# Two decoder layers on one core: first loads put in one queue, two modulation products moved, the attention output product split

## The reference

```python
c_act = silu(c)
for i in range(2):
    mod = c_act @ ada_w[i] + ada_b[i]                      # 6 x 1024
    shift_m, scale_m, gate_m, shift_f, scale_f, gate_f = split(mod, 6)
    h = rmsnorm(x, norm_g[i, 0]) * (1 + scale_m) + shift_m
    y = s5_mixer(h, ...) if i == 0 else stick_breaking_attention(h, w_qkv, w_out)
    x = x + gate_m * rmsnorm(y, norm_g[i, 1])
    h = rmsnorm(x, norm_g[i, 2]) * (1 + scale_f) + shift_f
    y = swiglu(h, ...) if i == 0 else moe_swiglu(h, ...)   # 8 experts, top 2
    x = x + gate_f * rmsnorm(y, norm_g[i, 3])
```

## Time and profile before

| | |
|---|---|
| Time before, median of 3 runs | 1456.86 us (1450.53 to 1460.29) |
| The profiled execution: device time | 1458.7 us |
| The profiled execution: span of its instructions | 1456.9 us |
| PE busy | 1336.3 us, 92% of the span |
| DVE / ACT / POOL busy | 657.1 / 510.7 / 41.7 us |
| DMA queue of SP (q1) | 470.83 MB, 78.3% of 16 engines' span |
| HBM read | 471.48 MB, 324 GB/s over the span |

### The profile page before, as it was taken

The page is one execution under the profiler, slowest core; times in us unless marked ns, Lnnn a source line. Parts: engine busy times, 40 slices in busy tenths (PEclk is TensorE's granted clock), DMA queues, the critical chain, the costliest instruction groups (busy, mean ns, idle before and its releaser), DMA issues.

```text
span 1456.9 us, 25193 instructions
## 1 busy us (share of the span) xinstructions
PE 1336.3 (92%) x11110; PEld 955.9 (66%) x11111; DVE 657.1 (45%) x738; ACT 510.7 (35%) x559; POOL 41.7 (3%) x80
## 2 busy tenths in 40 slices
PE   2999999999999888999999899999898899988776
PEld 1774678888779754677777677777676666644332
DVE  4943354444453444555554665554765463200002
ACT  1323433433344432444443444443454352000001
POOL 3000000000010003000000000000000000000000
PEclk8989999999999998999999999999999899999999
DMA  9573794555485305679999979999999999999994
GB/s 398 226 320 134 295 406 174 180 200 198 174 322 196 118 7 224 239 286 389 422 429 430 428 284 387 424 428 429 429 398 429 430 428 430 427 431 431 430 431 185
DMA packets 33371, 474.29 MB, mean 326 GB/s; under 512 B 3682, under 2 KB 3810, under 8 KB 4578
## 3 DMA queue, kind: packets, MB, share of 16 engines
q1 hardware_dynamic: 32544, 470.83, 78.3%
q10 hardware_dynamic: 706, 1.72, 0.3%
HBM read 471.48 MB, written 1.05 MB: 324 GB/s over the span
## 4 chain that ended last, share of the span: by engine, by line
PE 76%; DMA 17%; DVE 3%; ACT 2%; issue 1%; POOL 1%; ACTq 0%; POOLq 0%; SPq 0%; DVEq 0%
PE ps L2394 42%; PE ps L2725 10%; DMA ring<-in_moe_w_down_dram 8%; DMA ring<-in_moe_w_gate_up_dram 6%; PE ps L2737 6%; DMA arena<-in_s_cb_dram 2%; PE ps L2567 2%; PE ps L2370 2%; PE ps L2212 1%; DMA ring<-in_ada_w_dram 1%; PE ps L2717 1%; PE ps L2646 1%; PE ps L2269 1%; PE ps L2659 1%; PE ps L2707 1%
## 5 line engine op out<-in xcount | busy, mean ns | idle before, releaser
L1962 DVE TENSOR_TENSOR ring_lo<-ring,w 128x2048 fp32r<-128x2048 f32 x122 | 278.9, 2290 | 165.9 <-ACT w L1100 129.3
L1100 ACT ACTIVATE w<-ring 128x2048 fp32r<-128x2048 f32 x122 | 232.8, 1912 | 193.4 <-PE ps L2394 192.0
L2725 PE MATMUL ps<-ring,arena 128*32 128x128 f32 (+1 forms) x5376 | 239.3, 292 | 24.6 <-DMA ring<-in_moe_w_gate_up_dram 20.0
L2725 PEld LDWEIGHTS ps<-ring,arena 128*32 128x32 f32 (+1 forms) x5376 | 183.3, 114 | 84.5 <-DMA ring<-in_moe_w_gate_up_dram 30.4
L2394 PE MATMUL ps<-ring_lo,x_hi 128*128 128x512 f32 x576 | 224.7, 390 | 0.0
L1592 DVE TENSOR_TENSOR ring_lo<-ring,w_hi 128x2048 fp32r<-128x2048 f32 x42 | 95.6, 2290 | 86.5 <-ACT w_hi L822 86.5
L2394 PE MATMUL ps<-w,x_hi 128*128 128x512 f32 x320 | 128.8, 402 | 1.3 <-DVE arena L1914 1.1
L2394 PE MATMUL ps<-w,x_lo 128*128 128x512 f32 x320 | 124.8, 390 | 0.0
L2394 PEld LDWEIGHTS ps<-ring_lo,x_hi 128*128 128x128 f32 x576 | 108.3, 188 | 20.7
L822 ACT ACTIVATE w_hi<-ring 128x2048 fp32r<-128x2048 f32 x42 | 78.8, 1909 | 46.6 <-PE ps L2394 42.1
L2737 PE MATMUL ps<-ring,tri 128*32 128x512 f32 (+1 forms) x448 | 72.2, 650 | 23.0 <-DMA ring<-in_moe_w_down_dram 21.0
(11 more groups left out here) (397 smaller groups left out, 1695.2 us busy)
## 6 DMA issues: line engine op xcount, KB each, us to landing
ring<-in_moe_w_gate_up_dram SPq DMA_DIRECT2D x112, 2048.0 KB, 15.0
ring<-in_moe_w_down_dram SPq DMA_DIRECT2D x56, 2048.0 KB, 16.9
ring<-in_ada_w_dram SPq DMA_DIRECT2D x24, 2048.0 KB, 9.9
ring<-in_ffn_w_gate_up_dram SPq DMA_DIRECT2D x14, 2048.0 KB, 11.0
ring<-in_ffn_w_down_dram SPq DMA_DIRECT2D x7, 2048.0 KB, 8.6
ring<-in_sb_w_qkv_dram SPq DMA_DIRECT2D x6, 2048.0 KB, 8.7
ring<-in_s_w_out_dram SPq DMA_DIRECT2D x2, 2048.0 KB, 8.8
ring<-in_sb_w_out_dram SPq DMA_DIRECT2D x2, 2048.0 KB, 14.3
```

What stands on the lines that cost most here:

```text
L1100: act.activation(half3(h).bitcast(F32R), ff_half(gran(pair_place(*main_granule(n))), half), ACT.Copy).then_inc(whi_done, 1 + h if h and h ...
L1962: dve.tensor_tensor(ff_half(ring_lo[place % RING][:, :], half).bitcast(F32R), ff_half(gran(place), half), half3(h), ALU.subtract).then_inc ...
L2725: ins = pe.matmul(dst[width * r:width * r + width, 0:cols], x[:, k, 0:width], weights[:, k, cols * r:cols * r + cols], start=k == 0, stop= ...
```

## The change

Three places of the program are changed.

1. SP issues `x_sb` and then both S5 matrices (now one array of 128 x 1024, `cb`, one DMA) ahead of its first weight granule; ACT issues only `small` and the bias. The two blanks are ACT copies with scale 0 (`blank`) in place of POOL memsets. PE turns the groups of `bs` as 2, 4 and 2: two ahead of `ada_fold(1)`, two in the middle of `h @ w_in`. DVE starts the angles (two instructions) ahead of `hT_evict(0)`.
2. Between the S5 mixer and the FFN, `transpose_x(1)` goes ahead of `ada(6)`, which now uses PSUM bank 2 and whose fold goes into the FFN's first block; `ada(7)` and its fold go there too.
3. In the attention output product, three of four weight halves and `oT` are split; the first half of the first granule stays plain.

```diff
+            sp.dma_start(x_sb[:, :, :], x[0].rearrange("(t p) d -> p t d", p=P)).then_inc(x_in, 16)
+            sp.dma_start(cb, s5_cb).then_inc(cb_in, 16)
             for r in range(4):
...
-            pool.memset(ring[:, RING - 2, :], 0.0).then_inc(blank_done, 1)
-            pool.memset(resp.rearrange("p i t d h -> p (i t d h)"), 0.0).then_inc(blank_done, 1)
...
-            act.dma_start(x_sb[:, :, :], x[0].rearrange("(t p) d -> p t d", p=P)).then_inc(x_in, 16)
-            act.dma_start(cT.rearrange("p i t h -> p (i t h)"), s5_cb[0]).then_inc(cb_in, 16)
-            act.dma_start(b_raw.rearrange("p i t h -> p (i t h)"), s5_cb[1]).then_inc(cb_in, 16)
...
+            def blank(dst, columns):
+
+                src = ones[:, :].unsqueeze(1).to_broadcast([P, columns // P, P])
+                act.activation(dst.rearrange("p (a b) -> p a b", b=P), src, ACT.Copy, scale=0.0).then_inc(blank_done, 1)
+
+            blank(ring[:, RING - 2, :], GRAN)
...
+            blank(resp.rearrange("p i t d h -> p (i t d h)"), 2 * NT * (CHUNK + 1) * 32)
...
             ada_part(1)
+            wv_out(0, 2)
             ada_mod(1)
-            wv_out(0, 4)
+            wv_out(2, 4)
             hT_evict(0)
-            wv_out(4, 8)
+            wv_out(4, 6)
             u_raw_out(0)
+            wv_out(6, 8)
...
-            ada_part(7)
+            ada_part(6)
             for f in range(FB):
...
                 if f == 0:
-                    ada_mod(7)
+                    ada_mod(6)
                 silu_out(f, 1)
                 if f:
                     a_round(2 * f - 1, 0)
+                else:
+                    ada_part(7)
                 w_round(g + 1, 1)
+                if f == 0:
+                    ada_mod(7)
...
+            def s_round(h):
+
+                wait_landed(act, N_SBOUT + h // 2)
+                if h == 3:
+                    act.wait_ge(o_ps, HEADS // 2)
+                act.activation(half_s(h).bitcast(F32R), ff_half(gran(N_SBOUT + h // 2), h % 2), ACT.Copy
+                               ).then_inc(s_whi, 1)
...
+                if h == HEADS // 2:
+                    s_round(1)
...
+            o_round(0)
+            s_round(2)
+            o_round(1)
+            s_round(3)
             wait_used(act, N_SBOUT + 1)
...
+            angles(True)
             hT_evict(0)
-            angles()
+            angles(False)
...
+            s_rest(1)
             gate_diag(2)
+            o_rest(0)
+            o_rest(1)
+            s_rest(2)
             gate_copy(2)
+            s_rest(3)
...
+            pe.wait_ge(ct_done, 8)
+            turned_bs(0, 2)
             ada_fold(1)
...
+            turned_bs(2, 6)
             wait_hT(0)
...
                 if b == 1:
                     ins.then_inc(u_ps, 1)
+                    turned_bs(6, 8)
...
             ada_fold(4)
-            pe.wait_ge(mod_out, 5)
-            ada(6)
             ada_fold(5)
             transpose_x(1)
-            ada_fold(6)
-            pe.wait_ge(mod_out, 6)
-            ada(7)
+            ada(6)
             wait_hT(1)
...
                 if f == 0:
-                    ada_fold(7)
+                    ada_fold(6)
+                    ada(7)
...
                 if f == 0:
+                    ada_fold(7)
                     pe.wait_ge(mod_out, 8)
...
+            wait_landed(pe, N_SBOUT)
+            for tt in range(TT):
+                for k in range(KD // 2):
+                    pe.matmul(ps[:, Y_BANK + 2 * tt, :], oT[:, k, P * tt:P * tt + P], gran8(N_SBOUT)[:, k, :],
+                              start=k == 0, stop=False)
+            gate_row(2)
+            pe.wait_ge(s_olo, 2)
+            for h in range(1, 4):
+                r, half = divmod(h, 2)
+                pe.wait_ge(s_wlo, h)
```

More of the change, by code:

```diff
@@ L238, in program @@
         par = pl(42, NT)
-        cT = pl(2, NT, HG)
         rows = pl(640)
@@ L888, in _ @@
             ada_mod(5)
-            ada_part(6)
-            ada_mod(6)
             def a_round(q, ch):
@@ L974, in _, with o_round @@
                     act.preload_act_table_set("natural_log_exp_and_others")
+            def s_round(h):
[4 more added lines that the diff above has]
+                               ).then_inc(s_whi, 1)
+            def o_round(half):
+                k = slice(4 * half, 4 * half + 4)
+                act.wait_ge(o_done, 4 * half + 4)
+                act.activation(x_hi[:, k, :].bitcast(F32R), oT[:, k, :], ACT.Copy).then_inc(s_ohi, 1)
             for h in range(HEADS // 2 + 1):
                 b = h % 2
+                if h == HEADS // 2:
+                    s_round(1)
                 if h < HEADS // 2:
@@ L1426, in y_banks, with angles @@
                 return ps[:, Y_BANK + 2 * tt:Y_BANK + 2 * tt + 2, :].rearrange("p a b -> p (a b)")
-            def angles():
+            def angles(begin):
                 dve.wait_ge(turn_ready, 2)
@@ L1435, in angles @@
                 s, co = sinT, cosT
-                step(dve.tensor_tensor(s, t, fh, ALU.mult))
-                link(dve.tensor_tensor(co, t, fl, ALU.mult))
+                if begin:
+                    step(dve.tensor_tensor(s, t, fh, ALU.mult))
+                    link(dve.tensor_tensor(co, t, fl, ALU.mult))
+                    return
                 link(dve.tensor_scalar(scratch, s, MAGIC, MAGIC, ALU.add, ALU.subtract))
@@ L1710, in _, with s_rest, o_rest @@
             o_out(HEADS // 2 - 1)
+            def s_rest(h):
+                dve.wait_ge(s_whi, h)
+                dve.tensor_tensor(low_s(h).bitcast(F32R), ff_half(gran(N_SBOUT + h // 2), h % 2), half_s(h), ALU.subtract
+                                  ).then_inc(s_wlo, 1)
+            def o_rest(half):
+                k = slice(4 * half, 4 * half + 4)
+                dve.wait_ge(s_ohi, half + 1)
+                dve.tensor_tensor(x_lo[:, k, :].bitcast(F32R), oT[:, k, :], x_hi[:, k, :], ALU.subtract).then_inc(s_olo, 1)
+            s_rest(1)
             gate_diag(2)
+            o_rest(0)
+            o_rest(1)
+            s_rest(2)
             gate_copy(2)
+            s_rest(3)
             wait_used(dve, N_SBOUT + 1)
@@ L2252, in _, with turned_bs @@
             ada(1)
-            ada_fold(1)
-            pe.wait_ge(ct_done, 8)
-            for m in range(8):
-                i, q = divmod(m, TPB)
-                pe.wait_ge(bs_done, i + 1)
-                above(pe, wv_done, m - 1)
-                for t in range(TPB):
-                    ins = pe.transpose(ps[:, 2 + m % 2, P * t:P * t + P],
-                                       bs[:, i, TPB * q + t, :, :].rearrange("p d h -> p (d h)"), ident[:, :])
-                ins.then_inc(bt_ps, 1)
+            def turned_bs(lo, hi):
+                for m in range(lo, hi):
+                    i, q = divmod(m, TPB)
+                    pe.wait_ge(bs_done, i + 1)
+                    above(pe, wv_done, m - 1)
+                    for t in range(TPB):
+                        ins = pe.transpose(ps[:, 2 + m % 2, P * t:P * t + P],
+                                           bs[:, i, TPB * q + t, :, :].rearrange("p d h -> p (d h)"), ident[:, :])
+                    ins.then_inc(bt_ps, 1)
+            pe.wait_ge(ct_done, 8)
+            turned_bs(0, 2)
+            ada_fold(1)
+            turned_bs(2, 6)
             wait_hT(0)
@@ L2561, in _ @@
             pe.wait_ge(o_done, HEADS // 2)
-            for r in range(2):
-                n = N_SBOUT + r
-                wait_landed(pe, n)
-                for tt in range(TT):
-                    for k in range(KD):
-                        ins = pe.matmul(ps[:, Y_BANK + 2 * tt + r, :], oT[:, k, P * tt:P * tt + P], gran8(n)[:, k, :],
-                                        start=k == 0, stop=k == KD - 1)
-                    if r == 0 and tt == 0:
-                        gate_row(2)
-                ins.then_inc(used[n % RING], 1)
+            wait_landed(pe, N_SBOUT)
[8 more added lines that the diff above has]
+                pe.wait_ge(s_wlo, h)
+                hi, low = [w.rearrange("p (k n) -> p k n", n=512) for w in (half_s(h), low_s(h))]
+                for tt in range(TT):
+                    t = slice(P * tt, P * tt + P)
+                    for i in range(KD // 2):
+                        k = KD // 2 * half + i
+                        ins = split_product(ps[:, Y_BANK + 2 * tt + r, :], (x_hi[:, k, t], x_lo[:, k, t]),
+                                            (hi[:, i, :], low[:, i, :]), k == 0, k == KD - 1)
+                if half:
+                    ins.then_inc(used[(N_SBOUT + r) % RING], 1)
             ada(10)
@@ L3239, in laid_out @@
     b = [inputs[f"s5_b_{part}"][0].reshape(NT, 2, NS, HG).transpose(1, 2, 0, 3) for part in ("re", "im")]
-    s5_cb = np.stack([np.concatenate([w.reshape(P, NT * HG) for w in pair], axis=1) for pair in (c, b)])
+    s5_cb = np.concatenate([w.reshape(P, NT * HG) for w in c + b], axis=1)
     def by_columns(w, width):
```

13 lines of the change are left out of this document (10 added, 3 removed).

## The result

The changed kernel takes 1444.85 us (median of 17 runs, 1441.22 to 1450.35), the kernel before 1455.84 (17 runs beside them, 1448.44 to 1462.00). The ratio is 0.993, with a 95% interval from 0.9913 to 0.9947: 10.2 us less, between 7.7 and 12.7. That lies inside the range of 1433 to 1449, 4.85 us above the 1440 forecast. By the bound of 1% it is "within 1%" (chance 0.40) and not "faster" (0.57), which I had held the likelier, and the sum of 16.7 us lies outside the measured 7.7 to 12.7. The profiled execution has a span of 1440.4 us, 16.5 less than the profiled one of before and almost exactly that sum. The agreement is an accident in two ways. Two effects of about 6 us that the sum didn't have stand against each other in it, as the experiments show.

What follows compares the result with a forecast made beforehand. The prediction took the expert stretch as a fixed-length block, PE and weight stream tied together, hanging on the routing. From a median of 1456.86 us, -10.0 - 2.5 - 4.2 = -16.7 gave 1440.2, said as 1440, range 1433 to 1449.

Steps and rivals of the forecast that it cites:

- the bound of 1%: What a measurement of this kernel can tell from no change: 14.6 us, a time of 1442.3 us.
- the sum of 16.7 us: Whole kernel: gains of 10.0 at the start, 2.5 in the modulation products and 4.2 in the output product.
- Step 1, the start: Kernel start: x and matrices land earlier, `h @ w_in` starts 11.1 us earlier; -10.0 us after 1.1 for turning inside it.
- Rival C: Kernel start: landing order does not follow the queue, so the start gains nothing; 1450 us, chance 0.05.
- rival B: Start gives half, -6.5: `small` lands no earlier or `ada(1)` at low clock delays ACT; sum -13, 1444, chance 0.20.
- Step 2, the modulation: Between mixer and FFN: FFN starts 6.4 to 8.1 us earlier but takes on 4.8; net -2.5 us taken.
- Step 3, the output product: Attention output product: 24 of 32 matmuls split, 25.2 us for 29.46, -4.2 us.
- Behind it the same length: Expert stretch: routing comes 16 to 17 us earlier and the stretch behind it keeps its length.
- Rival F: Expert stretch lasts longer by what is saved, needing a stream ahead of the routing; no change, 1457, chance 0.03.
- Rival D: PE clock: idle at 27 to 33 us goes, low clock near 96 us later or shorter; 5 us more, 1435, chance 0.08.
- rule on transposes: Kernel start: transposes don't count as busy PE for the clock, so `h @ w_in` would begin at 1.2 GHz.

Runs made afterwards that it cites:

- experiment 8: Kernel before with only the loads of x and the S5 matrices moved first in SP's queue: 1447.40 us, ratio 0.9935.
- experiment 1: Kernel before with the start part alone (queue order, blanks on ACT, split turning of `bs`, earlier angles): 1440.67 us, ratio 0.9898.
- experiment 5: Kernel before with 49 fulfilled waits ahead of PE's first product, no work changed: 1467.15 us, ratio 1.0058.
- 6: Changed kernel with 209 fulfilled waits ahead of PE's first product, with its own 47 making a shift of 256: 1441.86 us, ratio 0.9907.
- 9: Changed kernel with 112 fulfilled waits ahead of `ada(0)`, branches 159 instructions further than before: 1437.64 us, ratio 0.9888.
- 12: Kernel before with the output product split alone and 110 fulfilled waits ahead of `ada(0)`: 1448.21 us, ratio 0.9937.
- experiment 2: Kernel before with the modulation part alone (x turned ahead of `ada(6)`, `ada(7)` inside the first FFN block): 1455.06 us, ratio 0.9999.
- 3: Kernel before with the split output product alone: 1457.74 us, ratio 1.0021.
- 7: Changed kernel with 197 fulfilled waits and three extra products into an unused bank ahead of `ada(1)`: 1446.49 us, ratio 0.9933.
- experiment 10: Changed kernel with 209 instructions at the end of an unexecuted body of the first expert pair, moving the branch target: 1444.59 us, ratio 0.9936.
- 11: Changed kernel with three extra products into an unused bank ahead of `ada(1)`, without added waits: 1448.13 us, ratio 0.9950.
- experiment 4: The whole changed kernel measured again beside its three parts on one chip, against the kernel before: 1445.15 us, ratio 0.9927.

## Why the prediction was right in time and wrong in its account

- **Step 1, the start: right.** x at 6.1 us (6.9 worked out), the matrices at 7.3 (8.1), `ada(1)` at 27.68 (27.9), `h @ w_in` at 39.53 (38.3, inside 37.3 to 39.8). Its end came 8.8 earlier where the sum has 10.0: `ada(1)` took 6.51 us, more than the 5.44 of the low clock in the earlier trace rows that I had taken as the worst. Rival C is refuted by experiment 8. The measured time is that of rival B (1444), but not for its reason: it had the start at -6.5, and PE's rows have -8.8. Its second half, a slow `ada(1)` that delays ACT, did happen and cost the 1.2 us.
- **Step 2, the modulation: too large.** -1.4 for -2.5 in the profile. Where the start part is there nothing of it is left: experiment 1, without the modulation part, reaches the third FFN product at 158.9, since `ada(7)` ran at the full clock there. The sum compared with products of 5.34 us in the earlier trace rows, whose length was the clock's and not the order's.
- **Step 3, the output product: right in its own rows**, 25.23 us for 25.2 and no wait. The price that the sum left out is what it adds to the instruction stream.
- **"Behind it the same length": the step that failed.** I took the expert stretch as a block of fixed length that hangs on the routing, so the sum put its change at nothing. It lost 6.5 us of the 23.0 in the profiles, about as much as the sum of 16.7 lies above the measured 10.2, though what part of that is the clock's isn't known. Rival F named that outcome, but for another reason, a weight stream running ahead, and SP's wait is still 25.8 us. What is shown: the large gaps come with 49 instructions and no other change (experiment 5) and go with a shift to 256 (6) or 159 (9, 12), and the small gap moves by half as many products as instructions were put ahead. That the gaps are fetches of instructions is inferred from this. The Trainium skill (Runtime: NRT & Kernel Launch, "Instruction fetch mechanics") says that instructions are refilled in blocks of 16 KiB, 256 of them, and that "Branching breaks sequential prefetch". The traces agree: the instruction queue moved 1.51 MB in 92 packets, 16.4 KB each, and 256 instructions bring the old gaps back. If so, the branch hints in the code hide the fetch only from some places.
- **The clock gave what the expert stretch took.** Rival D had its sign and size (5 us; it is 6.4), at the chance of 0.08, but its reason, the earlier start, isn't borne out: experiment 2 lacks the low clock with the old start, and experiment 8 has it with the new one. A low clock in the S5 stage stands in the profiles of before and of experiments 3, 5 to 8 and 10 to 12, and in none of after and of experiments 1, 2, 4 and 9. With the earlier start, all profiles in which `ada(1)` ran at the full clock have it (6, 7, 8, 10, 11), and all in which it ran at the low one, in whole (6.5 us: after, 1, 9) or in part (5.34 us: 4), lack it. That is a bond between two things of an execution, and no cause is shown: the changed kernel itself took both courses (6.51 in after, 5.34 in experiment 4, 3.64 in experiment 10, which is the same up to the experts), and experiment 2, with the old start and `ada(1)` at the low clock as in before, lacks the low clock that before has. In the times the start part gives 14.9 us, which fits best if most of its timed executions lacked the low clock and most of before's had it. So the 6.4 us are what this pair of profiles shows; how much of the 10.2 is the clock's stays open.
- The Trainium skill's rule on transposes (TensorE: Matmul & The Clock Gate, "Part 4: PE-mode transpose"), weighed against step 1: at 36 to 39 us PE mostly turned blocks, at a granted clock of 1.00, and `h @ w_in` began at the full clock. The rows don't show the rule's effect here.

In the profiles, the start gives 8.8, the clock in the S5 stage 6.4, the modulation 1.4, the output product 4.2 and the rest ahead of the experts 2.2, for the most part other stretches of clock, and the expert stretch takes 6.5. Without the clock the edits come to 7.9, against the 10.2 (7.7 to 12.7) of the times.

## What to carry to other kernels

Where an engine's stream is long and branches, every edit moves all branches behind it, and this can cost or give more than the edit itself: look for gaps ended by "issue" right behind a branch, and compare an edit at two or three places of the stream, made by fulfilled waits in idle time, before it is judged. Order the first loads by who waits for them: by PE's rows the queue alone gave nearly all of the start. And before a saving is read off two profiles, take out the stretches in which the granted clock differs, and see where in the spread of its kernel's times each profiled execution lies, or the clock's luck is booked as the edit's gain.

## What was not expected of the hardware

- 49 fulfilled waits in idle time made the kernel 8.4 us slower (1.0058), and 112 made the changed one 7 us faster. The largest gap at a branch was 3.34 us, and 3.90 for the block behind it.
- A fulfilled wait instruction costs PE 0.106 us: 209 of them end at 25.65 us, 197 at 24.38. At 112 they were hidden ahead of 17.16.
- With not one instruction different ahead of it, `ada(1)` took 6.51, 5.34 and 3.64 us in three executions. With the new start, profiles with 3.64 us had a low clock in the S5 stage (in experiment 10 it costs 4.8 us: from the start of `h @ w_in` to the stage's end 88.5 for 83.7) and the others had none; the cause isn't known.
